# Products of 64 rows or 64 columns issued in turn from the two halves of the TensorE array

## What is computed

```python
def nsa_compress(kv, pe, w1, w2):          # kv: 256 tokens, 2 groups, 64 wide
    idx = jnp.arange(n_c)[:, None] * NSA_CMP_STRIDE + jnp.arange(NSA_CMP_LEN)[None, :]
    blocks = kv[:, idx] + pe[None, None, :, None, :]
    blocks = blocks.transpose(0, 1, 3, 2, 4).reshape(B, n_c, G, NSA_CMP_LEN * D)   # n_c = 15, 2048 wide
    return jax.nn.silu(blocks @ w1) @ w2
...
        s = jnp.einsum("btgjd,bcgd->bgjtc", qb, kc) * scale
```

```python
    u = t_inv @ (vc * bc[..., None])
    w = t_inv @ (kb * jnp.exp(gcum)[..., None])
    ...
    def step(state, xs):
        v_new = u_i - w_i @ state
```

## Time and profile before

| | |
|---|---|
| median of 3 runs | 1213.13 us (1210.08 to 1213.62) |
| the profiled execution's own time | 1207.15 us |
| its span | 1205.4 us |
| mean granted TensorE clock | 0.951 |
| PE busy | 1033.0 us (86%) |
| PEld busy | 541.0 us (45%) |
| DVE busy | 435.3 us (36%) |
| ACT busy | 240.4 us (20%) |
| read from HBM | 321.47 MB, mean 268 GB/s |

### The profile page before, as it was taken

One profiled execution on the slowest core, in us unless ns is written; L12 is line 12 of the kernel. 1 busy time (PEld: TensorE's weight loads), 2 busy tenths in 40 slices (PEclk: granted clock), 3 DMA queues, 4 the chain that ended last, 5 costly groups with the idle time before them and its releaser, 6 DMA issues.

```text
span 1205.4 us, 18371 instructions
## 1 busy us (share of the span) xinstructions
PE 1033.0 (86%) x7810; PEld 541.0 (45%) x7810; DVE 435.3 (36%) x1031; ACT 240.4 (20%) x590; POOL 55.1 (5%) x70
## 2 busy tenths in 40 slices
PE   5999999999999989999998889898675666766666
PEld 2345764444577446885676765432111111211111
DVE  0138646423855527345348773411000000000002
ACT  0012144111213513445112251200000000000002
POOL 0101000000100000001212400000000000000000
PEclk9999999999989999999999999899989888879789
DMA  9963348443325984013322015999999999999996
GB/s 385 411 268 140 117 148 334 171 157 140 140 88 233 429 367 157 1 70 147 134 73 73 4 71 217 418 407 433 428 428 432 430 429 431 429 428 430 430 431 281
DMA packets 28160, 323.69 MB, mean 269 GB/s; under 512 B 3264, under 2 KB 3392, under 8 KB 5808
## 3 DMA queue, kind: packets, MB, share of 16 engines
q1 hardware_dynamic: 26048, 314.18, 63.6%
q0 software_dynamic: 2032, 8.35, 1.9%
HBM read 321.47 MB, written 1.05 MB: 268 GB/s over the span
## 4 chain that ended last, share of the span: by engine, by line
PE 58%; DMA 33%; DVE 5%; issue 2%; SPq 1%; ACT 1%; DVEq 0%; ACTq 0%
PE banks L650 48%; DMA ring<-in_stream 17%; DMA zuv_to_Kt<-in_stream 15%; PE banks L661 3%; PE banks L913 1%; SPq L553 1%; PE banks L934 1%; PE banks L2219 1%; PE banks L899 1%; PE banks L896 1%; PE banks L800 1%; DVE KC L1249 0%; PE banks L904 0%; PE banks L937 0%; DVE probs L1299 0%
## 5 line engine op out<-in xcount | busy, mean ns | idle before, releaser
L650 PE MATMUL banks<-ring,uT 128*128 128x512 f32 (+1 forms) x512 | 225.8, 595 | 7.3 <-DVE uT L1116 3.0
L650 PEld LDWEIGHTS banks<-ring,uT 128*128 128x128 f32 x512 | 96.3, 192 | 121.1 <-issue 114.0
L650 PE MATMUL banks<-scr_qk 64*64 64x64 f32 (+4 forms) x2368 | 97.3, 266 | 25.8 <-DMA scr_qk<-in_stream 19.0
L650 PE MATMUL banks<-ring,scr_qk 128*32 128x512 f32 (+1 forms) x496 | 85.1, 642 | 28.4 <-DMA ring<-in_stream 27.7
L2790 DVE SCALAR_TENSOR_TENSOR UWK<-UWK,banks 128x256 f32<-128x256 f32 x16 | 6.7, 421 | 263.8 <-ACT UWK L3076 263.8
L650 PE MATMUL banks<-ring,UWK 128*32 128x512 f32 (+1 forms) x336 | 85.4, 768 | 12.8 <-ACT UWK L3084 9.2
L650 PEld LDWEIGHTS banks<-scr_qk 64*64 64x64 f32 (+3 forms) x2368 | 70.0, 135 | 54.3 <-issue 41.8
L3076 ACT ACTIVATE UWK<-banks 128x256 f32<-128x256 f32 x16 | 6.1, 384 | 361.1 <-PE banks L650 361.1
L650 PE MATMUL banks<-UWK,ring 128*128 128x256 f32 x320 | 71.0, 380 | 0.0
L2219 PE MATMUL banks<-UWK 128*128 128x512 f32 x128 | 65.3, 633 | 0.9 <-DVE UWK L2798 0.9
L650 PEld LDWEIGHTS banks<-UWK,ring 128*128 128x128 f32 x320 | 60.4, 190 | 9.3 <-issue 1.4
(11 more groups left out here) (384 smaller groups left out, 1223.4 us busy)
## 6 DMA issues: line engine op xcount, KB each, us to landing
ring<-in_stream SPq DMA_DIRECT2D x93, 2048.0 KB, 14.7
scr_qk<-in_stream SPq DMA_DIRECT2D x11, 2048.0 KB, 40.0
Vt_to_O<-in_stream SPq DMA_DIRECT2D x11, 2048.0 KB, 39.5
zuv_to_Kt<-in_stream SPq DMA_DIRECT2D x10, 2048.0 KB, 39.2
scr_qk<-in_stream SPq DMA_DIRECT2D x11, 1024.0 KB, 41.2
wide<-in_stream SPq DMA_DIRECT2D x10, 1024.0 KB, 38.8
const<-in_stream SPq DMA_DIRECT2D x10, 1024.0 KB, 37.5
misc<-in_stream SPq DMA_DIRECT2D x10, 1024.0 KB, 39.4
```

Source lines behind the costliest of these rows:

```text
L650: return pe.matmul(o, a, b, start=start, stop=stop)
```

## The change

The three places issue the same products in another order, the two halves in turn. In `pe_cmp1` moreover the result of v = 1 goes to partitions 64 to 127 of bank 3, so that keys and values lie in different column halves; ACT and DVE read them there, and DVE writes `hid2` to partitions 0 to 63 as before. The waits for the two banks stand together ahead of the first product in `pe_cmp1` and in `pe_cmp_s`. Nothing is added or taken out.

```diff
--- before.py
+++ after.py
@@ -828,12 +828,14 @@
         def pe_cmp1(pe, l):
             pe.wait_ge(*at("cmpw", l))
             pe.wait_ge(*at("blocks", l))
-            for v in range(2):
-                pe.wait_ge(*free(2 + v))
-                for a in range(LPAIR):
-                    ins = mm(pe, bank[2 + v][0:HD, 0:2 * N_CMP], w1[:, v, a, :],
+            pe.wait_ge(*free(2))
+            pe.wait_ge(*free(3))
+            for a in range(LPAIR):
+                for v in range(2):
+                    ins = mm(pe, bank[2 + v][HD * v:HD * v + HD, 0:2 * N_CMP], w1[:, v, a, :],
                              blk[:, v, a, :, :].rearrange("p g c -> p (g c)"), a == 0, a == LPAIR - 1)
-                ins.then_inc(*fill(2 + v, "cmp1", l, v))
+                    if a == LPAIR - 1:
+                        ins.then_inc(*fill(2 + v, "cmp1", l, v))
 
         def pe_cmp2(pe, l):
             pe.wait_ge(*free(2))
@@ -849,14 +851,16 @@
             pe.wait_ge(*at("KCT", l))
             pe.wait_ge(*at("turned", l, 4))
             pe.wait_ge(*at("turned", l, 5))
-            for b in range(2):
-                pe.wait_ge(*free(6 + b))
-                for h in range(b, NSA_H, 2):
-                    for t in range(TILES):
-                        c = (h // 2 * TILES + t) * N_CMP
-                        ins = mm(pe, bank[6 + b][:, c:c + N_CMP], TB[HD * b:HD * b + HD, B_NQ + h // 2, t * P:(t + 1) * P],
-                                 KCT[HD * b:HD * b + HD, h // HPG, :], True, True)
-                ins.then_inc(*fill(6 + b, "cmp_s", l, b))
+            pe.wait_ge(*free(6))
+            pe.wait_ge(*free(7))
+            for i in range(NSA_H // 2):
+                for t in range(TILES):
+                    c = (i * TILES + t) * N_CMP
+                    for b in range(2):
+                        ins = mm(pe, bank[6 + b][:, c:c + N_CMP], TB[HD * b:HD * b + HD, B_NQ + i, t * P:(t + 1) * P],
+                                 KCT[HD * b:HD * b + HD, (2 * i + b) // HPG, :], True, True)
+                        if (i, t) == (NSA_H // 2 - 1, TILES - 1):
+                            ins.then_inc(*fill(6 + b, "cmp_s", l, b))
 
         def pe_cmp_pT(pe, l):
             pe.wait_ge(*at("PC", l))
@@ -1305,8 +1309,8 @@
             for v in range(2):
                 dve.wait_ge(*at("hid_tanh", l, v))
                 dve.wait_ge(*at("cmp1", l, v))
-                dve.scalar_tensor_tensor(hid2[0:HD, v, :], hid[0:HD, v, :], 1.0,
-                                                   bank[2 + v][0:HD, 0:2 * N_CMP], ALU.add, ALU.mult).then_inc(*drain(2 + v, "hid", l, v))
+                dve.scalar_tensor_tensor(hid2[0:HD, v, :], hid[HD * v:HD * v + HD, v, :], 1.0,
+                                                   bank[2 + v][HD * v:HD * v + HD, 0:2 * N_CMP], ALU.add, ALU.mult).then_inc(*drain(2 + v, "hid", l, v))
                 dve.wait_ge(*drained(2 + v))
 
         def v_cmp_kv(dve, l):
@@ -1589,7 +1593,7 @@
         def a_cmp_hid(act, l):
             for v in range(2):
                 act.wait_ge(*at("cmp1", l, v))
-                act.activation(hid[0:HD, v, :], bank[2 + v][0:HD, 0:2 * N_CMP], ACT.Tanh, scale=0.5).then_inc(*tick("scalar_step", "hid_tanh", l, v))
+                act.activation(hid[HD * v:HD * v + HD, v, :], bank[2 + v][HD * v:HD * v + HD, 0:2 * N_CMP], ACT.Tanh, scale=0.5).then_inc(*tick("scalar_step", "hid_tanh", l, v))
                 act.wait_ge(*last("scalar_step"))
 
         def a_gates(act, l):
@@ -1950,12 +1954,12 @@
                         ins.then_inc(*fill(4 * t + i // 4, "U_mm", s, t, i // 4))
                 pe.wait_ge(*at("bK", s, t))
                 bK = scr[:, t, Y_:T_ + 1, :].rearrange("p a n -> p (a n)")
-                for p in (0, CH):
-                    for i in range(NDH):
-
+                for i in range(NDH):
+                    for p in (0, CH):
                         ins = mm(pe, bank[4 * t + 2 + p // CH][:, i * CH:(i + 1) * CH], bK[p:p + CH, i * P:(i + 1) * P],
                                  scr[p:p + CH, t, TT_, i * CH:(i + 1) * CH], True, True)
-                    ins.then_inc(*fill(4 * t + 2 + p // CH, "W_mm", s, t, p // CH))
+                        if i == NDH - 1:
+                            ins.then_inc(*fill(4 * t + 2 + p // CH, "W_mm", s, t, p // CH))
 
         def at_step(n, r):
 
```

## The result

| | before | after |
|---|---|---|
| median | 1213.13 us (1210.08 to 1216.2, 5 runs) | 1196.62 us (1196.0 to 1198.75, 5 runs) |
| profiled execution's own time | 1207.15 us | 1196.62 us |
| span | 1205.4 us | 1194.8 us |

The two profiled executions are 10.5 us apart, the medians 16.5; these two differences are not the same, and that turned out to be the clue.

What follows compares the result with a forecast made beforehand. PE was taken to bound the kernel, with DMA bursts starting as PE frees slots; 5.5 (W) + 1.8 (scores) + 0 (first layer) = 7.3 us, so 1213.1 - 7.3 = 1205.8 us; 8-in-10 range 1200.5 to 1211.

Steps and rivals of the forecast that it cites:

- The bound: Whole kernel: PE time saved ahead of 380 and 745 us starts both DMA bursts as much earlier, their length kept.
- The W products: 128 W matmuls ahead of the recurrence: row halves overlap, 54 ns a step, 5.5 us less for four tiles.
- The scores: Scores of the compression: 54 ns a step in turn, 0.9 us less a layer, 1.8 us in all.
- The first layer: Compression's first layer: 29 ns a step, but nothing starts before bank 3 is free at 121.14; no gain.
- DVE's copy: Copy of the W product, 0.70 us, already on the path: next to be late, and included in the sum.
- the term for the clock: Layer 1's 1.2 GHz stretches, in the compression and behind its scores, costing 3.4 and 1.7 us: both left in the sum.
- the step from the profiled execution to the median: Median taken as 6 us above the profiled execution with the same work, so 7.3 us came off 1213.1.
- Clock no longer falls in layer 1: Rival: compression and scores packed tighter keep layer 1's clock up; 5.1 us less, 1200.7 us; chance 0.10.
- Clock falls in layer 0 too: Rival: PE's 2.3 us idle ahead of layer 0's compression lowers its clock; costs 3.4 us, 1209.2 us; chance 0.10.
- Column halves do not overlap: Rival: compression's first layer stays at 59 ns a step, 3.7 us lost, 1209.5 us; chance 0.08.
- W's gain is lost: Rival: another wait, DVE or a DMA burst, ends last behind PE; only 1.8 us stay, 1211.3 us; chance 0.06.
- slower: Rival: switching halves keeps loads in W and scores from being pulled ahead; 10.1 us more, 1223.2 us; chance 0.04.

Runs made afterwards that it cites:

- the trace at hand: Kernel before, unchanged: the profiled execution the forecast was made from; 1207.15 us by its own time, span 1205.4 us.
- all three: Changed kernel again (also called the other comparison), against the kernel before on one chip: 1198.52 us against 1211.36, ratio 0.9885.
- the wait alone: Kernel before with only the wait for bank 3 moved ahead of the compression's first product, no halves in turn: 1222.85 us, ratio 1.0084 to before.
- the same column half: Changed kernel with keys and values of the compression's first layer in turn in one column half: 1210.22 us, ratio 0.9971 to the kernel before.
- the first comparison: Changed kernel, all three places, against the kernel before: 1196.62 us against 1213.13, ratio 0.9869.

## Why the prediction was wrong, point by point

**What was right.** The bound (PE early, one burst of DMA at the end that starts as much earlier as PE does): the profiled execution's gain at the recurrence is carried to the end (11.8 us at its first product, 10.6 in the span; the difference is in part a slow stretch at 684). The W products: 5.5 us forecast, 13.6 - 8.0 = 5.6 measured. The scores: 1.8 forecast, 4.9 - 3.0 = 1.9. The first layer: no gain forecast, none measured (ratio 1.0009 alone), with the step of 29 ns and the wait for bank 3 as reckoned. DVE's copy stayed the next thing on the path. The 5.5 us of W and the 1.8 of the scores were sound, and the miss does not come from them.

**What was wrong: the term for the clock, and the step from the profiled execution to the median.** The step that failed is the sum's treatment of the clock: the prediction left both slow stretches of layer 1 in it, at a change of 0, "as the change alters what lies ahead in both ways". In its place the traces show 6.1 us less lost to the clock, over four of each kernel. It also overlooked the stretch at 171.6 in layer 0's attention, which lies ahead of the last burst as well. And it said the median was "6 us above it, with the same work", and took the same 7.3 us off it. The 6 us were not a constant: the trace at hand was an execution with fewer slow stretches than the three others (13.7 us of them ahead of 740 where the others have 30.7, none from 620 to 740 where the others have 0.93 or 0.94), and a good part of what sets a typical execution above it is what the change takes away. For the profiled execution itself the forecast was 1199.9, and 1196.6 came out, 3.3 us less: by the chain, the slow stretches at 171.6 and 362.7 are gone and that at 332 is half as long (1.7 us each), and one in the recurrence is new. (A further new one, at 636, did not lengthen the way from the one W copy to the other.)

**The rivals.** "Clock no longer falls in layer 1" (0.10) came nearest with 1200.7, but it is only partly right: behind the scores of layer 1 the clock stayed up in all four traces of the changed kernel, in the compression of layer 1 it fell in all four. And it left out the W products, which lost clock in three executions that the trace at hand did not show. "Clock falls in layer 0 too" did happen in two of the four traces of the changed kernel (from 121.7 and from 121.0), against one of the four of before (from 123.0); it costs part of what the scores and W give back. "Column halves do not overlap" is refuted by the 29 ns, and with it the rule of the Trainium skill ("TensorE: Matmul & The Clock Gate", "The mechanism") that a load overlaps only with matmuls of another row group: the trace disagrees. In the same column half the step is 58 ns. "W's gain is lost" and "slower" did not come about.

**What is shown and what stays open.** That the lengths alone are too few is shown by the medians: at least 9.8 us for all three, at least 6.7 us lost for a wait of 3.7. That the rest is the clock is shown by the time at 1.2 GHz in the traces, which brings the two kernels to 6.4 us apart, and the wait alone and the same column half to within 1 us of their lengths. Where the clock is kept rests on counting: behind the scores 12 of 14 against 3 of 14, in the W group of s = 1 never in seven. It is less clear for the whole stretch from 620 to 740: of the seven traces with the old order of W four have 0.93 or 0.94, but three have 0.97 to 1.00, the wait alone among them with 0.99; of the seven with the new order none is below 0.97. Each variant has one trace only, and one cause moving all of it in time, so that slow stretches fall elsewhere, isn't excluded. How much of the 16.5 us of the first comparison above 13.4 is chance isn't settled either; the other comparison's interval (0.9852 to 0.9919) holds both.

## What to carry to other kernels

Two products that use different halves of the array (rows or columns) and are issued in turn go at half the step, where weight loads set the pace (111 to 54 ns, 58 to 29 ns here); but place the waits of both ahead of both only where PE has something else to do meanwhile. Where the work on PE is short and thin (few moving columns, pauses), count its clock as part of its cost, and look at several traces before taking the difference between a profiled execution and the median for a constant: it may be the very thing the change removes.

## What the runs showed of the hardware that was not expected

- Weight loads into different column halves overlap as fully as into different row halves: 29 ns a step against 58 in the same half (64 columns), and 54 against 111 for row halves (128 columns).
- A wait of 2.4 us ahead of thinly filled products brought PE to 1.2 GHz in or at the start of them in 12 of 14 cases; at its worst 64 matmuls took 6.97 us instead of 3.8.
- With the same products issued in turn instead of half by half the clock fell less often: behind the scores in 3 of 14 cases instead of 12 of 14. Whether the scatter of the times shrinks with it isn't shown: 13 us over 29 runs of the kernel before, but 8 us over all 8 of the changed one on the same chip.
